# The down product moved into its own item's turn, with down weights loaded an expert ahead

## What is computed

```python
logits = ht @ w_router + b_router
top_val, top_idx = lax.top_k(logits, 4)          # 4 of 32 experts for each of 256 tokens
gates = softmax(top_val)
def expert_block(xblk, e):                        # for the tokens that chose expert e
    gu = xblk @ w_gate_up[e] + b_gate_up[e]       # [1024] -> [2048]
    gate = minimum(gu[:, :1024], 7.0)
    up = clip(gu[:, 1024:], -7.0, 7.0)
    act = gate * sigmoid(1.702 * gate) * (up + 1)
    return act @ w_down[e] + b_down[e]            # [1024] -> [1024]
out[token] = sum over its experts of gate * expert_block(...)
```

## Time and profile before

| | us |
|---|---|
| median of 3 runs (1388.44 to 1391.1) | 1389.85 |
| the profiled execution | 1391.75 |
| its span (what the profile covers) | 1390.0 |
| TensorE busy in the span | 1159.7 (83%) |
| VectorE / ScalarE busy | 278.1 / 217.7 |
| DMA: bytes moved, mean rate | 458.17 MB, 330 GB/s |
| TensorE's mean granted clock, share of 2.4 GHz | 0.876 |

### The profile page before, as it was taken

How to read it: one execution, slowest core, us unless ns; L and a number is a source line. 1 busy time by engine, 2 the same in 40 slices (tenths; PEclk the granted TensorE clock), 3 DMA queues, 4 the chain that set the end, 5 groups by cost and what they waited for, 6 DMA issues and landing times.

```text
span 1390.0 us, 29000 instructions
## 1 busy us (share of the span) xinstructions
PE 1159.7 (83%) x11279; PEld 558.6 (40%) x11280; DVE 278.1 (20%) x806; ACT 217.7 (16%) x486; POOL 78.3 (6%) x197
## 2 busy tenths in 40 slices
PE   4989998898899677667799999977768789769994
PEld 1768885563544122122244444422113334324441
DVE  0254523223511001000121212110001111101212
ACT  2221122112211011000111111110001111101111
POOL 8000000002000000000000000000000000000000
PEclk9999998658899878777899999987778989979996
DMA  9432119516789999999979998999999997999175
GB/s 354 177 121 92 62 62 338 208 62 239 301 347 422 422 422 422 422 422 422 414 313 422 422 402 334 422 422 421 422 422 422 422 422 298 423 422 422 63 322 237
DMA packets 81263, 458.17 MB, mean 330 GB/s; under 512 B 6950, under 2 KB 8064, under 8 KB 32048
## 3 DMA queue, kind: packets, MB, share of 16 engines
q1 hardware_dynamic: 79280, 452.00, 79.9%
q0 software_dynamic: 1440, 5.13, 1.1%
q10 hardware_dynamic: 512, 0.60, 0.1%
HBM read 455.58 MB, written 2.11 MB: 329 GB/s over the span
## 4 chain that ended last, share of the span: by engine, by line
PE 54%; DMA 22%; SPq 15%; DVE 3%; issue 2%; ACT 2%; ACTq 1%; DVEq 0%
DMA raw<-in_w_down 20%; PE bank L1769 16%; PE bank L1782 9%; SPq L350 9%; PE bank L1349 7%; SPq L354 5%; PE bank L1811 3%; PE bank L1678 2%; PE bank L1742 2%; PE bank L1314 2%; PE bank L1791 2%; DMA odd<-in_w_gate_up 1%; PE bank L1499 1%; PE bank L1758 1%; PE bank L1502 1%
## 5 line engine op out<-in xcount | busy, mean ns | idle before, releaser
L1782 PE MATMUL bank<-raw,aT 128*32 128x256 f32 x3328 | 240.3, 436 | 73.6 <-DMA raw<-in_w_down 71.0
L1769 PE MATMUL bank<-raw,xT 128*32 128x512 f32 x1600 | 212.3, 658 | 54.8 <-DMA raw<-in_w_gate_up 38.2
L1769 PE MATMUL bank<-odd,xT 128*32 128x512 f32 x1664 | 209.3, 632 | 34.1 <-DMA odd<-in_w_gate_up 34.1
L1782 PEld LDWEIGHTS bank<-raw,aT 128*32 128x32 f32 x3328 | 113.4, 121 | 211.7 <-DMA raw<-in_w_down 124.2
L1253 DVE TENSOR_TENSOR gated<-bank,bias_i 128x256 f32<-128x256 f32 x51 | 21.7, 425 | 748.8 <-PE bank L1791 748.8
L1769 PEld LDWEIGHTS bank<-raw,xT 128*32 128x32 f32 x1600 | 49.4, 115 | 182.4 <-DMA raw<-in_w_gate_up 90.7
L1349 PE MATMUL bank<-hT,raw 128*128 128x256 f32 (+1 forms) x496 | 116.6, 395 | 2.4 <-ACT hT L570 2.4
L1769 PEld LDWEIGHTS bank<-odd,xT 128*32 128x32 f32 x1664 | 48.3, 112 | 156.5 <-DMA odd<-in_w_gate_up 76.4
L1349 PEld LDWEIGHTS bank<-hT,raw 128*128 128x128 f32 (+1 forms) x496 | 95.2, 195 | 21.2 <-issue 5.8
L517 POOL TENSOR_TENSOR gatehot<-onehot,gates 128x128 f32<-128x128 f32 x102 | 38.5, 399 | 944.9 <-PE bank L1758 923.3
L768 ACT ACTIVATE evy<-bank 128x256 f32<-128x256 f32 x52 | 19.9, 383 | 450.3 <-PE bank L1782 450.3
(11 more groups left out here) (380 smaller groups left out, 893.4 us busy)
## 6 DMA issues: line engine op xcount, KB each, us to landing
raw<-in_w_gate_up SPq DMA_DIRECT2D x128, 1024.0 KB, 21.9
raw<-in_w_down SPq DMA_DIRECT2D x128, 1024.0 KB, 18.4
odd<-in_w_gate_up SPq DMA_DIRECT2D x128, 1024.0 KB, 25.8
raw<-in_w_ada SPq DMA_DIRECT2D x12, 2048.0 KB, 9.4
raw<-in_w_in SPq DMA_DIRECT2D x7, 2048.0 KB, 8.0
raw<-in_w_out SPq DMA_DIRECT2D x2, 2048.0 KB, 10.8
raw<-in_w_in SPq DMA_DIRECT2D x1, 1056.0 KB, 5.3
x_sb<-in_x SPq DMA_DIRECT2D x1, 1024.0 KB, 5.0
```

The source lines that it names most:

```text
L1769: g = mm(bank[0][j * CAP:(j + 1) * CAP, :], xT[:, u % 2, u // 2, :], gu_slab(u, p)[:, j * NC:(j + 1) * NC], start=u == 0, stop=u == KT - 1)
L1782: g = mm(bank[1][j * CAP:(j + 1) * CAP, 0:NQ], aT[:, k % 4, k // 4, :], dn_slab(u)[:, at:at + NQ], start=k == 0, stop=k == KT - 1)
```

## The change

`down(i)` is run in item i's own turn, after `gather`, `turn`, `scatter`, `turn_gates`, `turn_tokens` and `scatter_rest`; the half-and-half split of the gate-up goes. `turn(i)` moves from the end of the turn to right behind `gather`. The `down` of item -1 and the one behind the last item go.

Down pieces 0 to 2 get a second set of buffers (`dn2`), so SyncE's list becomes, for each e: down pieces 0 to 2 of expert e (each behind a wait for `down` of expert e-2), then all 8 slabs of gate-up of expert e+1 (each behind a wait for the gate-up of expert e-1). Piece 3 keeps one buffer and is loaded from ScalarE's queue, by `last_slab`, behind the last item of the expert before. For this, ScalarE's list becomes a loop over experts with a loop over items in it. ScalarE's `sigmoid` stands ahead of `take_xT`, and VectorE's minimum with LIMIT ahead of the `ups` addition.

```diff
         def dn_done(i, u):
-            return S("dn_mm"), 4 * (i + 1) + u + 1
+            return S("dn_mm"), 4 * i + u + 1
...
-        def dn_slab(u):
-            return ring_half(8 + u)
+        def dn_slab(u, p):
+            return dn2[u][:, :] if p and u < 3 else ring_half(8 + u)
+        def dn_in(u, p):
+            return S(f"dn_loaded{u}_{p}" if u < 3 else "dn_loaded3")
...
+            for u, done in enumerate(((S("x1_ready"), 4), (S("ss_ready"), 2 * TT), (S("items_ready"), 5))):
+                sp.wait_ge(*done)
+                load_dn(sp, 1, u, 1)
+            def next_gu(e, before, p):
+                for u in range(KT):
+                    sp.wait_ge(*gu_done(before, u))
+                    load_gu(sp, e + 1, u, p)
+            def next_dn(e, before, p):
+                for u in range(3):
+                    sp.wait_ge(*dn_done(before, u))
+                    load_dn(sp, e, u, p)
+            next_gu(1, before, 0)
+            with sp.Fori(1, NE // 2 - 1) as q:
                 for p in range(2):
-                    e = 2 * q + 1 + p
-                    before = sp.value_load(last_item[0:1, bass.ds(e - 1, 1)], min_val=0, max_val=NI)
-                    for u in range(4):
-                        sp.wait_ge(*gu_done(before, u))
-                        load_gu(sp, e + 1, u, p)
-                    for u in range(4):
-                        sp.wait_ge(*dn_done(before, u))
-                        load_dn(sp, e, u)
-                    for u in range(4, 8):
-                        sp.wait_ge(*gu_done(before, u))
-                        load_gu(sp, e + 1, u, p)
+                    e = 2 * q + p
+                    before = sp.value_load(last_item[0:1, bass.ds(e - 2, 1)], min_val=0, max_val=NI)
+                    next_dn(e, before, p)
+                    before = sp.value_load(last_item[0:1, bass.ds(e - 1, 1)], min_val=0, max_val=NI)
+                    next_gu(e, before, 1 - p)
...
             def item(i):                       # ScalarE
                 take_gu(i)
                 take_xg(i + 1)
+                sigmoid(i)
                 take_xT(i + 1)
                 take_scat(i)
-                sigmoid(i)
+                take_y(i)
+            def last_slab(e, after):
+                act_e.wait_ge(S("dn_mm"), 4 * after)
+                load_dn(act_e, e + 1, 3, 0)
...
             def join(i, body):                 # VectorE
...
+                body.wait("gate")
+                ts(gated[:, :, :, :], gated[:, :, :, :], LIMIT, None, ALU.min).then_inc(S("gate_ready"), 1)
                 tt(ups[:, :, :, :], turned[:, :, 2:4, :],
                    bias_i[:, :, 2:4].unsqueeze(3).to_broadcast([P, 4, 2, CAP]), ALU.add).then_inc(S("tr_ev"), 1)
             def act(i, body):
-                body.wait("gate")
-                ts(gated[:, :, :, :], gated[:, :, :, :], LIMIT, None, ALU.min).then_inc(S("gate_ready"), 1)
...
                     with pe.Fori(first, after) as i:          # TensorE
-                        gate_up(i, 0, p, q)
-                        before = pe.value_load(items[0:1, bass.ds(i, 1)], min_val=0, max_val=NE - 1)
-                        for u in range(1, 4):
-                            gate_up(i, u, p, q)
-                        down(i - 1, before)
-                        for u in range(4, 8):
+                        for u in range(KT):
                             gate_up(i, u, p, q)
                         gather(i + 1)
+                        turn(i)
                         scatter(i - 1)
                         turn_gates(i)
                         turn_tokens(i + 1)
                         scatter_rest(i - 1)
-                        turn(i)
-            down(n_it - 1, NE - 1)
+                        down(i, p, q)
```

More of the change, by code:

```diff
@@ L121, in build @@
         SLOT = 4096
-        moe = Region(base + 21 * SLOT)
+        moe = Region(base + 23 * SLOT)
         xT = moe("xT", [P, 2, CT, CAP])
@@ L125, in build @@
         xg = moe("xg", [P, NQ])
-        evg = moe("evg", [P, NC])
         evy = moe("evy", [P, NQ])
-        onehot = moe("onehot", [P, TT, CAP])
         gatehot = moe("gatehot", [P, TT, CT, CAP])
-        scat = moe("scat", [P, T])
         gated = moe("gated", [P, 4, 2, CAP])
@@ L133, in build @@
         ups = moe("ups", [P, 4, 2, CAP])
+        assert moe.at <= base + 25 * SLOT
+        evg = place("evg", [P, NC], F32, base + 16 * SLOT + SLOT // 2)[0]
+        moe = Region(base + 27 * SLOT)
+        scat = moe("scat", [P, T])
+        onehot = moe("onehot", [P, TT, CAP])
         bias_i = moe("bias_i", [P, 4, 4])
-        assert moe.at <= base + 25 * SLOT
+        dn2 = [place(f"dn2_{u}", [P, 2 * D], F32, base + n * SLOT)[0] for u, n in enumerate((19, 21, 25))]
         def at_slot(n, name, shape, dt=F32, off=0):
@@ L342, in gu_slab, with load_dn @@
             return odd[u][:, :] if p else ring_half(u)
-        def dn_slab(u):
-            return ring_half(8 + u)
+        def dn_slab(u, p):
+            return dn2[u][:, :] if p and u < 3 else ring_half(8 + u)
+        def dn_in(u, p):
+            return S(f"dn_loaded{u}_{p}" if u < 3 else "dn_loaded3")
         def load_gu(sp, e, u, p):
             sp.dma_start(gu_slab(u, p), gu_src(e, u)).then_inc(S(f"gu_loaded{u}_{p}"), 16)
-        def load_dn(sp, e, u):
-            sp.dma_start(dn_slab(u), dn_src(e, u)).then_inc(S(f"dn_loaded{u}"), 16)
+        def load_dn(sp, e, u, p):
+            sp.dma_start(dn_slab(u, p), dn_src(e, u)).then_inc(dn_in(u, p), 16)
         last = raw[:, RING_ORDER[0], :, :].rearrange("p k n -> p (k n)")
@@ L393, in _ @@
                 else:
-                    load_dn(sp, 0, cc - KT)
+                    load_dn(sp, 0, cc - KT, 0)
             free = {17: (S("wo_mm"), 4), 6: (S("h2_ready"), TT), 8: (S("h2_ready"), TT), 14: (S("bias_T"), 1),
@@ L399, in _ @@
                 load_gu(sp, 1, u, 1)
-            sp.wait_ge(S("items_ready"), 5)
-            with sp.Fori(0, NE // 2 - 1) as q:
+            for u, done in enumerate(((S("x1_ready"), 4), (S("ss_ready"), 2 * TT), (S("items_ready"), 5))):
[9 more added lines that the diff above has]
+                    load_dn(sp, e, u, p)
+            before = sp.value_load(last_item[0:1, 0:1], min_val=0, max_val=NI)
+            next_gu(1, before, 0)
+            with sp.Fori(1, NE // 2 - 1) as q:
                 for p in range(2):
-                    e = 2 * q + 1 + p
+                    e = 2 * q + p
+                    before = sp.value_load(last_item[0:1, bass.ds(e - 2, 1)], min_val=0, max_val=NI)
+                    next_dn(e, before, p)
                     before = sp.value_load(last_item[0:1, bass.ds(e - 1, 1)], min_val=0, max_val=NI)
-                    for u in range(4):
-                        sp.wait_ge(*gu_done(before, u))
-                        load_gu(sp, e + 1, u, p)
-                    for u in range(4):
-                        sp.wait_ge(*dn_done(before, u))
-                        load_dn(sp, e, u)
-                    for u in range(4, 8):
-                        sp.wait_ge(*gu_done(before, u))
-                        load_gu(sp, e + 1, u, p)
+                    next_gu(e, before, 1 - p)
+            before = sp.value_load(last_item[0:1, NE - 4:NE - 3], min_val=0, max_val=NI)
+            next_dn(NE - 2, before, 0)
+            before = sp.value_load(last_item[0:1, NE - 3:NE - 2], min_val=0, max_val=NI)
+            next_gu(NE - 2, before, 1)
+            next_dn(NE - 1, before, 1)
             before = sp.value_load(last_item[0:1, NE - 2:NE - 1], min_val=0, max_val=NI)
-            for u in range(4):
-                sp.wait_ge(*dn_done(before, u))
-                load_dn(sp, NE - 1, u)
             sp.wait_ge(*gu_done(before, 1))
@@ L763, in take_y @@
             def take_y(i):
-                act_e.wait_ge(S("dn_mm"), 4 * (i + 1) + 4)
-                if not isinstance(i, int) or i >= 0:
-                    act_e.wait_ge(S("scattered"), i + 1)
+                act_e.wait_ge(S("dn_mm"), 4 * i + 4)
+                act_e.wait_ge(S("scattered"), i + 1)
                 a.activation(evy[:, :], bank[1][:, 0:NQ], ACT.Copy).then_inc(S("y_ev"), 1)
@@ L772, in take_gu @@
                 act_e.wait_ge(S("gu_mm"), 8 * i + 8)
-                if not isinstance(i, int):
-                    act_e.wait_ge(S("turned"), i)
+                act_e.wait_ge(S("turned"), i + 1)
                 a.activation(evg[:, :], bank[0][:, :], ACT.Copy).then_inc(S("gu_ev"), 1)
@@ L811, in _ @@
             act_e.wait_ge(S("items_ready"), 5)
[L812 to L818, removed]
+            with act_e.Fori(0, NE // 2 - 1) as q:
+                after = act_e.value_load(first_item[0:1, bass.ds(2 * q, 1)], min_val=0, max_val=NI)
+                for p in range(2):
+                    first, e = after, 2 * q + p
+                    after = act_e.value_load(first_item[0:1, bass.ds(e + 1, 1)], min_val=1, max_val=NI)
+                    with act_e.Fori(first, after) as i:
+                        item(i)
```

(28 more changed lines are left out.)

## The result

The change made the kernel faster by 1.5%: 1369.91 us (median of 4 runs, 1366.54 to 1371.24) against 1389.94, a ratio of 0.9855 with a 95% interval of 0.984 to 0.987. I had forecast 1348 and a range of 1336 to 1364; the gain is 20 us, not 42. The profiled execution took 1370.19 us, its span 1367.7.

What follows compares the result with a forecast made beforehand. DMA loads and TensorE bound the kernel alternately. Pauses of 31.2 us shrink to 3, so DMA is 28 us earlier at expert 28; with the end stretch the gain is 41.9 us: 1348 us, forecast 1342 to 1354, range 1336 to 1364.

Steps and rivals of the forecast that it cites:

- The first, second and fourth pause: DMA pauses at 400 to 407, 694 to 715 and 1160 to 1181 us, costing 5.4, 8.6, 9.2 us; all to go.
- `last_slab` and ScalarE's extra loop: ScalarE work between take_y and take_gu, during gate-up: cost nothing, up to a microsecond or two a loop covered.
- whose cover is now `gather` alone: Ahead of turn: the 0.6 us copy to evg starts with gather and ends 0.2 us ahead of it.
- The open wait: TensorE idle ahead of down, waiting for aT: 2.5 us chain less 1.8 us cover, taken as 0.6 us an item.
- the third pause: DMA pause at 823 to 844 us, costing 8.0 us; forecast to shrink to 3 us, near 817 to 820.
- the end stretch: From the last slab of expert 28's first item, forecast at 1203.1 us, eight items of 14.47 us, ending at 1331.2.
- The held-up issue: Rival: a full ring holds up ScalarE's DMA issue and take_gu, idle time ahead of evg; 1365 to 1400 us, chance 0.05.
- A wait twice as long: Rival: TensorE's wait ahead of down is 1.2 us an item; 1359 us, chance 0.18.
- The late piece: Rival: the fourth down piece from ScalarE's queue lands 22 us after issue, stalling first items; 1430 us, chance 0.06.
- TensorE's clock: Rival: holes in each item lower TensorE's clock, half the end stretch at 1.2 GHz; 1388 us, chance 0.03.
- More goes than I count: Rival: wait ahead of down is 0.3 us and no DMA pause is left; 1340 us, chance 0.10.

Runs made afterwards that it cites:

- e4: Also called experiment 3: the changed kernel's loads and buffers with TensorE's order of the kernel before, plus a sigmoid ahead of ScalarE's loop; 1345.31 us, ratio 0.969.
- e5: TensorE's order of the changed kernel with the kernel before's loads, single down buffers and flat ScalarE loop; 1404.97 us, ratio 1.0113.
- e1: The changed kernel plus one single-column sigmoid on ScalarE ahead of its loop over experts; 1358.13 us, ratio 0.9778.
- e6: The kernel before with the four down pieces moved behind gate-up slabs 4 to 7 in SyncE's list, no buffer added; 1396.85 us, ratio 1.0042.
- e2: On top of e1, GpSimd waits for aT of the item before it makes the next gatehot; 1353.0 us, ratio 0.9742.
- e3: On top of e1, the fourth down piece is loaded from SyncE's list behind the eight gate-up slabs, not from ScalarE's queue; 1409.26 us, ratio 1.0159.

## Why the prediction was wrong

**Right: what bounds, and which pauses go.** The first, second and fourth pause went. The experiments split the change: the new loads alone bring 44 us (e4 against the kernel before), the order alone costs 16 (e5), on top of the new loads it costs 13 (e1 against e4, where the small differences named under experiment 3 are part of the 13). The stall behind a wait for a down was real, and a new list alone (e6) doesn't remove it. Whether four doubled pieces in SyncE's list would do without the second queue wasn't tested.

**The step that failed.** It is "`last_slab` and ScalarE's extra loop stand between `take_y` and `take_gu` [...] cost nothing". The DMA issue did cost nothing (0.34 us). But the loop made its first function's table unknown, and the load went in behind `take_gu`'s wait, not before it: 1.27 us in 24 items (16.03 us against 14.76). The prediction's allowance there, "up to a microsecond or two a loop is covered", fails with it. Beside it stands "`turn` itself waits for `evg`, whose cover is now `gather` alone [...] ends 0.2 us ahead": I saw that the cover was 0.2 us, and didn't ask what could lengthen what it covers. Experiment 1 puts it at 10 to 12 us.

**The open wait.** Forecast 0.6 us, measured 0.81 (with GpSimd beside VectorE), 0.60 once GpSimd is kept away (e2). The term was right for the chain in the earlier trace rows, where GpSimd had nothing to do; in the changed order `turn_gates` starts GpSimd in the midst of VectorE's chain, so it was mis-sized by 0.2 us. Over the 8 last items and the 10 before the third pause that would be 4 us; experiment 2 gives 2.6 to 5.

**The sum, gone through with the rows of after.** To the third pause: expert 10's first item ended at 671 (forecast 670). Ten items followed, six even at 16.03 and four odd at 14.76, 155.2 us, and two turns of the loop at 1.1; expert 14's third item began at 829.1, against 816.5. DMA came to the pause at 813.9 (forecast 816.9). Hence 17.7 us of pause and not 3, ended 12 us later than forecast; the short pauses near 862 and 894 us add 3.7. That moved the anchor of the end stretch: expert 28's last slab started at

```profile
1218.87 1.94 PE L1802 MATMUL bank<-raw,xT 128*32 128x512 f32 x8 [0.55 <-DMA raw<-in_w_gate_up]
```

against 1203.1 forecast, 15.8 later. From there to the end of the last `down` (1349.65 + 1.05 = 1350.70) are 131.8 us, forecast 128.1: eight items longer by 0.29 us, and one table load, of expert 28's second item. Together 19.5 us, of 20.3 between the two profiled executions (1370.19 against 1349.9).

**What stays open.** Experiment 2 has the forecast's wait and no table loads, and is still 5 us above 1348. Its pause is 8.0 us (0.42 x 19) and not 3. Its items (14.55 us) and the loop's turn behind an odd expert (1.1 us and not 0.9) explain little of that. Most lies in the forecast's starting points: the DMA engines run dry 142.9 us after the end of expert 10's first item in the changed kernel (813.9 against 671.0) and in experiment 2 (818.3 against 675.4), where I had 146.9 (816.9 against 670). Part of these 4 us is a misreading: I took the pauses by the busy share, but by the rate (66 and 227 of 422 GB/s) the first two cost 5.9 and 9.7 us, not 5.4 and 8.6, which brings DMA 1.6 us earlier. The rest isn't explained.

**The rivals.** The held-up issue (0.05 of the chances) is the only one whose range, 1365 to 1400, holds the measured time, and its sign, time lost ahead of `evg`, is what the rows show; but the issue took 0.34 us, and what held up `evg` was the table load. A wait twice as long (1359) had the wrong cause: the added time lay mostly ahead of `turn`. The late piece didn't happen, and e3 shows that it was worth fearing. TensorE's clock didn't fall: 1.00 in each stretch shown above from 694 to 833 us, with 0.8 to 2 us of holes in an item, and 1.00 again from 1289 to 1350. The prediction read the holes of the earlier trace rows wrongly: in that stretch TensorE waits three times for VectorE, 2.28 us each, and never for DMA. "More goes than I count" had no pause left; the third pause grew instead.

## What to carry to other kernels

When a product is moved next to what feeds it, the whole feeding chain loses its cover, so each instruction of it must be priced as the new program will run it: a loop put around ScalarE's work can bring table loads, and an engine that this same step sets off can slow another. Make the table known ahead of a loop with one small activation. Take doubled buffers and a new order apart: here the new loads (buffers, list and second queue together) brought 44 us and the order cost 13, and the kernel with the new loads and the old order, at 1345 us, beats both versions. One late load can be passed ahead through a second queue even though all queues share one rate.

## What the hardware showed that I hadn't expected

A table load stands in front of the waiting activation only once its wait has ended (741.22, just behind the last gate-up slab), so that the idle 7.85 us before it didn't hide it; the groups put all 24 loads at `evg` behind that wait. VectorE's product of two SBUF tiles went from 0.42 to 0.62 us and GpSimd's pair from 0.76 to 1.08 when they ran together. ScalarE's 1 MB, beside a full SyncE queue, moved at 28% against 73% of the engines' time and landed in 9.1 us.
